# Linear attention's decay levels as differences of one running sum on GpSimd, and the samples' query latents for two heads per product

## What is computed

```python
log_a = jax.nn.log_sigmoid(glr @ w_gate_up + b_gate) / GLA_TAU
...
b = jnp.cumsum(gc, axis=2)
o_inter = jnp.einsum('bhcd,bhde->bhce', qc * jnp.exp(b), state)
diff = b[:, :, :, None, :] - b[:, :, None, :, :]
dec = jnp.exp(jnp.where(causal[None, None, :, :, None], diff, -jnp.inf))
att = jnp.einsum('bhid,bhjd,bhijd->bhij', qc, kc, dec)
...
new_state = jnp.exp(b_last[:, :, 0, :])[..., None] * state + jnp.einsum('bhcd,bhce->bhde', kc * jnp.exp(b_last - b), vc)
...
q_lat = jnp.einsum('bshn,rhn->bshr', q_nope, w_uk)
```

## Time and profile before

| | |
|---|---|
| three timed runs | 752.32, 753.34 (median), 758.79 us |
| the profiled execution | 748.42 us, its span 746.6 us |
| busy share of the span | PE 95%, PE weight load 73%, DVE 48%, ACT 43%, POOL 10% |
| chain that ended last | PE 91%, DVE 3%, ACT 2% |
| granted tensor clock, mean | 0.985 |

### The profile page before, as it was taken

One profiled execution on the slowest core, in us unless ns is written; L12 is line 12 of the kernel. 1 busy time (PEld: TensorE's weight loads), 2 busy tenths in 40 slices (PEclk: granted clock), 3 DMA queues, 4 the chain that ended last, 5 costly groups with the idle time before them and its releaser, 6 DMA issues.

```text
span 746.6 us, 16661 instructions
## 1 busy us (share of the span) xinstructions
PE 706.7 (95%) x7015; PEld 547.9 (73%) x7015; DVE 356.2 (48%) x782; ACT 324.1 (43%) x771; POOL 75.6 (10%) x113
## 2 busy tenths in 40 slices
PE   2899999999999989998899999999999999999995
PEld 1487878788789986776676577676668999668884
DVE  0454370030202024778665766665661112379977
ACT  1244650121212135765566655655757666602100
POOL 0000000000000010101121122012113443000000
PEclk9899999999999997999999999999999999999998
DMA  9996300303001020000010200020655885103332
GB/s 296 396 352 186 113 1 1 113 0 96 0 2 56 2 63 23 15 16 10 10 11 1 46 12 2 1 58 8 217 194 182 288 290 194 60 1 115 119 134 84
DMA packets 35301, 70.31 MB, mean 94 GB/s; under 512 B 6626, under 2 KB 17979, under 8 KB 33564
## 3 DMA queue, kind: packets, MB, share of 16 engines
q1 hardware_dynamic: 30602, 47.73, 19.7%
q0 software_dynamic: 4016, 20.97, 8.0%
q10 hardware_dynamic: 610, 0.55, 0.3%
HBM read 62.26 MB, written 6.07 MB: 92 GB/s over the span
## 4 chain that ended last, share of the span: by engine, by line
PE 91%; DVE 3%; ACT 2%; issue 1%; DMA 1%; ACTq 1%; POOL 0%; DVEq 0%; POOLq 0%
PE banks L2011 15%; PE banks L2023 12%; PE banks L2215 8%; PE banks L2343 5%; PE banks L2424 4%; PE banks L2444 4%; PE banks L2191 3%; PE banks L2577 2%; PE banks L2579 2%; PE banks L2578 2%; PE banks L2129 2%; PE banks L2032 2%; PE banks L2517 2%; PE banks L2536 2%; PE banks L2560 2%; PE banks L2561 1%
## 5 line engine op out<-in xcount | busy, mean ns | idle before, releaser
L1260 ACT ACTIVATE s_z<-banks 128x512 f32<-128x512 f32 (+1 forms) x88 | 41.4, 518 | 48.2 <-PE banks L2424 48.0
L1436 DVE COPY s_zs<-banks 8x512 f32<-8x512 f32 (+3 forms) x6 | 3.5, 576 | 118.5 <-PE banks L1985 118.4
L2011 PE MATMUL banks<-s_w_parts,s_h_b 128*128 128x256 f32 (+3 forms) x296 | 55.5, 315 | 0.0
L1041 ACT ACTIVATE s_z<-banks 128x416 f32<-128x416 f32 (+3 forms) x32 | 14.8, 475 | 92.3 <-PE banks L2011 92.3
L1251 ACT ACTIVATE s_z<-banks,s_temps 128x128 f32<-128x128 f32 (+7 forms) x64 | 47.1, 740 | 5.4 <-DVE s_temps L1738 5.0
L2011 PEld LDWEIGHTS banks<-s_w_parts,s_h_b 128*128 128x128 f32 x296 | 43.3, 189 | 3.6 <-issue 1.7
L2424 PEld LDWEIGHTS banks<-s_ident,s_z 128*128 128x128 f32 x288 | 33.4, 141 | 11.5 <-issue 5.8
L2023 PE MATMUL banks<-s_h_a,s_z_r 128*128 128x512 f32 x128 | 40.8, 395 | 0.0
L2023 PE MATMUL banks<-s_h_b,s_z_r 128*128 128x512 f32 x128 | 40.3, 393 | 0.0
L2424 PE MATMUL banks<-s_ident,s_z 128*128 128x128 f32 x288 | 39.8, 274 | 0.1
L2215 PE MATMUL banks<-s_kt,s_temps 96*128 96x512 f32 (+1 forms) x96 | 39.4, 532 | 0.0
(11 more groups left out here) (401 smaller groups left out, 1569.1 us busy)
## 6 DMA issues: line engine op xcount, KB each, us to landing
s_z<-in_w_ada SPq DMA_DIRECT2D x16, 512.0 KB, 12.1
s_temps<-in_w_in SPq DMA_DIRECT2D x3, 2048.0 KB, 7.9
s_x<-in_x_prompt SPq DMA_DIRECT2D x8, 512.0 KB, 12.0
s_z<-in_w_ada SPq DMA_DIRECT2D x1, 4096.0 KB, 14.1
s_kt<-in_w_out SPq DMA_DIRECT2D x8, 512.0 KB, 4.7
s_temps<-in_x_prompt SPq DMA_DIRECT2D x8, 512.0 KB
out_y_prompt<-s_temps SPq DMA_DIRECT2D x7, 512.0 KB
s_temps<-in_w_in SPq DMA_DIRECT2D x2, 832.0 KB, 14.0
```

The lines of the kernel that those rows point to most:

```text
L1260: nc.scalar.activation(PTb[r % 3][:, 4 * g:4 * g + n, :], banks[:, 4 + (groups(r) + g) % 2, 0:P * n].rearrange("p (j q) -> p j q", j=n), A ...
L2011: last = nc.tensor.matmul(banks[:, proj_bank(c, t), 0:WIDTH[c]], h_[half][:, k, n0:n0 + P], w_, start=(k == 0 and n == 0), stop=(k == KT - ...
```

## The change

The seven levels and the running sum are no longer products. `decay_sums` makes the running sum and the sum behind each token, from `la` itself in fp32: two products of 128 columns by `upto` and one of 256. ScalarE's `sums_out` copies the running sum to SBUF (`cum`) and exponentiates both. GpSimd's `differences` subtracts: per level two operations of 128 elements, the middle's value less the key half, and the query half less the middle's. ScalarE's `levels_out` exponentiates them in place, four levels and then three. The decays and sums have two buffers each. The running sum of block k+2 is now made in iteration k, behind the far products. The gate's bank is 0 from block 2 on, the latent keys' bank is 7. `S` and `attm` are cleared by VectorE. The transfer of the table and its conversion go.

In the samples, `w_uk` is turned for two heads at once (`wT`), the queries of two heads lie in the two halves of the rows with zeros between, and `qlat` is one product for two heads. There is one piece fewer.

```diff
-        ref = col // (2 * s) * (2 * s) + s - 1
-        sums[:, lv] = np.where((col // s) % 2 == 0, (col < row) & (row <= ref), (ref < row) & (row <= col))
-    sums[:, LEVELS] = row <= col
-    c["sums"] = sums.reshape(P, -1)
+    c["upto"] = (row <= col).astype(np.float32)
...
-        k_rows = [carve(256, region=act_flat) for _ in range(2)]
-        ckvT.append(carve(P, region=act_flat))
+        es = [carve((LEVELS + 1) * 256, LEVELS + 1, 2, P, region=act_flat) for _ in range(2)]
+        k_rows = [sb(f"k_rows{i}", [P, 256])[:] for i in range(2)]
...
+            def differences(t):
+                pool.wait_ge(cum_ready, t + 1)
                 if t > 1:
+                    pool.wait_ge(x_ready, t - 1)
+                for lv in range(LEVELS):
+                    n = P >> (lv + 1)
+                    b = halves_of(cum[t % 2], n)
+                    e = halves_of(es[t % 2][:, lv, :, :].rearrange("p h i -> p (h i)"), n)
+                    middle = b[:, :, 0, n - 1:n].to_broadcast([P, P // n, n])
+                    nc.gpsimd.tensor_tensor(e[:, :, 0, :], middle, b[:, :, 0, :], ALU.subtract)
+                    last = nc.gpsimd.tensor_tensor(e[:, :, 1, :], b[:, :, 1, :], middle, ALU.subtract)
+                    if lv in (FIRST_LEVELS - 1, LEVELS - 1):
+                        last.then_inc(diff_ready, 1)
             pool.wait_ge(proj_done, T * (NCH - 1))
             nc.gpsimd.memset(glT, 1.0).then_inc(padded, 1)
-            nc.gpsimd.tensor_copy(after_r, after[:]).then_inc(tables_ready, 1)
-            decay_parts(0)
-            pool.wait_ge(sums_in, 16)
-            nc.gpsimd.tensor_copy(sums, sums_raw).then_inc(tables_ready, 1)
-            decay_parts(1)
-            pool.wait_ge(proj_done, T * NCH)
-            nc.gpsimd.memset(S, 0.0).then_inc(padded, 1)
-            nc.gpsimd.memset(attm, 0.0).then_inc(padded, 1)
-            for t in range(2, T):
-                decay_parts(t)
+            for t in range(T):
+                differences(t)
             pool.wait_ge(kv_out, 32)
...
+            def sums_out(t):
+                act.wait_ge(sums_done, t + 1)
+                if t > 1:
+                    act.wait_ge(diff_ready, 2 * (t - 1))
+                    act.wait_ge(kdec_ready, t - 1)
+                nc.scalar.activation(cum[t % 2], banks[:, 0, 0:256], ACT.Copy).then_inc(cum_ready, 1)
+                nc.scalar.activation(es[t % 2][:, LEVELS, :, :].rearrange("p h i -> p (h i)"), banks[:, 0, 0:256], ACT.Exp, scale=1.0 / TAU).then_inc(sums_ready, 1)
+                nc.scalar.activation(esuf[t % 2], banks[:, 0, 256:512], ACT.Exp, scale=1.0 / TAU).then_inc(sums_ready, 1)
+            def levels_out(t, part):
+                act.wait_ge(diff_ready, 2 * t + part + 1)
+                v = es[t % 2][:, FIRST_LEVELS * part:(FIRST_LEVELS, LEVELS)[part], :, :].rearrange("p l h i -> p (l h i)")
+                nc.scalar.activation(v, v, ACT.Exp, scale=1.0 / TAU).then_inc(e_ready, 1)
...
+                    nc.vector.memset(S, 0.0).then_inc(padded, 1)
+                    nc.vector.memset(attm, 0.0).then_inc(padded, 1)
                     dve.wait_ge(padded, 6)
+                dve.wait_ge(sums_ready, 2 * t + 2)
                 if t > 1:
                     dve.wait_ge(o_done, t - 1)
                     dve.wait_ge(state_done, t - 1)
-                nc.vector.tensor_tensor(qb[t % 2], es[:, LEVELS, :, :].rearrange("p h i -> p (h i)"), kq(t)[:, 256:512], ALU.mult).then_inc(qb_ready, 1)
...
                 if t == 1:
-                    pe.wait_ge(k_copied, 2)
+                    pe.wait_ge(a_copied, 3)
                 for q in range(3):
                     nc.tensor.transpose(banks[:, 6, P * q:P * q + P], z[:, t, P * q:P * q + P], ident[:])
                 nc.tensor.transpose(banks[0:QK, 6, 384:512], z[:, t, W_KR - NOPE:W_GM], ident[:]).then_inc(a_transposed, 1)
             def latent_keys(t):
-                pe.wait_ge(a_copied, 3 * t + 3)
+                pe.wait_ge(a_copied, 3 * t + 1)
+                if t == 0:
+                    pe.wait_ge(la_ready, 2)
+                else:
+                    pe.wait_ge(k_copied, 2 * t)
                 for m in range(H // 2):
-                    last = nc.tensor.matmul(banks[:, 6, P * m:P * m + P], w_uk[:, P * m:P * m + P], turned_latents(t), start=True, stop=True)
+                    last = nc.tensor.matmul(banks[:, 7, P * m:P * m + P], w_uk[:, P * m:P * m + P], turned_latents(t), start=True, stop=True)
                 last.then_inc(k_done, 1)
...
+                nc.tensor.matmul(banks[:, gate_bank(t), 256:512], glT, w_gu[:], start=True, stop=True).then_inc(gate_done, 1)
+            def decay_sums(t):
+                pe.wait_ge(la_ready, t + 1)
+                if t > 0:
+                    pe.wait_ge(sums_ready, 2 * t)
+                for hp in range(2):
+                    nc.tensor.matmul(banks[:, 0, P * hp:P * hp + P], la[t % 2][:, P * hp:P * hp + P], upto[:], start=True, stop=True)
+                nc.tensor.matmul(banks[:, 0, 256:512], after[:], la[t % 2], start=True, stop=True).then_inc(sums_done, 1)
...
+                        if t == 3:
+                            decay_sums(0)
                         if t == 4:
                             key_rows(0)
                         if t == 5:
-                            decays(0, 0)
-                            decays(0, 1)
                             key_rows(1)
+                            decay_sums(1)
                         if t == 6:
-                            decays(0, 2)
-                            decays(0, 3)
-                            decays_after(0)
+                            latent_rows(0)
                             gate_rows(2)
-            latent_rows(0)
             latent_keys(0)
             pe.wait_ge(proj_copied, T * NCH)
             pe.wait_ge(padded, 6)
...
-                if n in (PREP["wT0"], PREP["wT1"]):
-                    for h in range(4):
-                        c0 = NOPE * (4 * (n - PREP["wT0"]) + h)
-                        last = nc.tensor.transpose(banks[0:NOPE, 7, P * h:P * h + P], w_uk[:, c0:c0 + NOPE], ident[:])
+                if n == PREP["wT"]:
+                    for m in range(H // 2):
+                        last = nc.tensor.transpose(banks[:, 7, P * m:P * m + P], w_uk[:, P * m:P * m + P], ident[:])
                 if n == PREP["qT"]:
                     pe.wait_ge(p_q4, 4)
                     for h in range(H):
-                        nc.tensor.transpose(banks[0:NOPE, 7, NB * h:NB * h + NB], sq[:, QK * h:QK * h + NOPE], i8)
+                        rows, c0 = slice(NOPE * (h % 2), NOPE * (h % 2) + NOPE), NB * (h // 2)
+                        nc.tensor.matmul(banks[rows, 7, c0:c0 + NB], sq[:, QK * h:QK * h + NOPE], i8, start=True, stop=True)
                     for h in range(H):
                         last = nc.tensor.transpose(banks[:, 7, 64 + NB * h:64 + NB * h + NB], sq4[:, h, :, :].rearrange("p a e -> p (a e)"), i8)
                 if n == PREP["qlat"]:
-                    for h in range(H):
-                        last = nc.tensor.matmul(banks[:, 7, NB * h:NB * h + NB], w_ukT[:, h, :], s_ql[:, h, :], start=True, stop=True)
+                    for m in range(H // 2):
+                        last = nc.tensor.matmul(banks[:, 7, 2 * NB * m:2 * NB * m + 2 * NB], w_ukT[:, m, :], s_ql[:, m, :, :].rearrange("p a b -> p (a b)"),
+                                                start=True, stop=True)
                 if n == PREP["init"]:
                     for b in range(NB):
                         nc.tensor.matmul(banks[0:32, 7, b:b + 1], qlw[:, b, 24:56], knT[:, b:b + 1], start=True, stop=False)
```

More of the change, by code:

```diff
@@ L246, in hybrid_step @@
         la = [carve(256) for _ in range(2)]
-        la_hi, la_lo = ([carve(256, region=C_parts) for _ in range(2)] for _ in range(2))
-        after_r = carve(P, region=C_parts)
+        cum = [carve(256) for _ in range(2)]
         xs = carve(LEVELS * 256, LEVELS, 256)
-        esuf = carve(256)
+        esuf = [carve(256) for _ in range(2)]
+        ckvT = [carve(P) for _ in range(2)]
         assert taken[0] <= B
-        ckvT = [carve(P)]
         attm = carve(512, 2, 2, P)
@@ L299, in hybrid_step @@
         s_cqT = carve(2 * 32, 2, 32)
-        s_ql = carve(H * NB, H, NB, rows=NOPE)
+        s_ql = carve(H * NB, H // 2, 2, NB)
         s_decT = carve(2 * NB, 2, NB)
@@ L326, in hybrid_step @@
         s_ss = sb("s_ss", [NB, 8])
-        w_ukT = carve(H * P, H, P, rows=NOPE)
+        w_ukT = carve(H // 2 * P, H // 2, P)
         assert taken[0] <= MLA_AT
@@ L619, in turned_latents, with gate_bank @@
             return ckvT[t % 2] if t < SOON else ckvT_late[:, t - SOON, :]
+        def gate_bank(t):
+            return 7 if t < 2 else 0
+        FIRST_LEVELS = 4
         def late_at(s):
```

188 lines of the change are left out of this document (68 added, 120 removed).

## The result

| kernel | time, median us | over the kernel before, 95% interval |
|---|---|---|
| before | 752.83 (749.21 to 758.79, 4 runs) | |
| changed | 760.02 (758.04 to 763.01, 4 runs) | 1.009 (1.0045 to 1.0134) |
| changed, second series (10 runs) | 760.08 | 1.0091 (1.0055 to 1.0127) |

The change costs 0.9%, 6.8 us, where 4.6 less were forecast: outside the range, on the wrong side. The profiled execution of the changed kernel took 759.15 us, 757.3 its span. The page: products went, and TensorE's busy time with them (706.7 to 698.6 us), but the span grew by 10.7, so the engine stands idle instead.

The account below looks back on a forecast made before the run. In the loop TensorE, VectorE and ScalarE were taken as near their limits, with VectorE's ring binding after the change. -1.1 - 2.3 - 3.4 + 3.5 - 0.8 - 0.5 = -4.6 us, from 753.3 to 748.7; range 739.0 to 758.5.

Parts of the forecast that it names:

- (1): Projections: block 0's sums go, the new sums of blocks 0 and 1 come in at 1.0 us each; -1.1 us.
- (2): Entry to the linear-attention loop: TensorE's waits of 0.93 and 1.39 us for ScalarE's copies go; -2.3 us.
- (3): Loop iteration k = 0: full clock wins 2.4 us, products removed 1.0; -3.4 us, to 11.4.
- (4): Loop iterations 1 to 5: VectorE and GpSimd collide, 62.9 us against 59.4; +3.5 us.
- The late ring: Loop, k = 3 to 5: VectorE's queue, each part waiting for the one before, takes 12.3 us per iteration.
- the collision: Loop: VectorE's two-SBUF-input products and GpSimd's differences take turns, 0.60 us a pair against 0.34 for VectorE's products alone.
- The ring of 13.0: Loop, k = 1 and 2: 3.1 us of ScalarE replace log decay and near pairs in VectorE's ring; 13.0 us each.
- (5): Samples' query latents: transposes and latent product records go, narrow products come in; -0.5 us, from -1 to 0.
- No collision: Rival, loop: VectorE and GpSimd do not hold each other up, -5.5 us instead of +3.5; 739.7 us, chance 0.14.
- Dearer GpSimd: Rival, loop: narrow GpSimd operations cost 0.73 us, a pair 0.87, adding 9.5 us; 758.2 us, chance 0.18.
- The clock falls inside the loop: Rival: TensorE's waits, mostly ahead of near products, lower the clock, six falls of 2.4 us; 763.1 us, chance 0.06.
- The entry stays slow: Rival, loop entry: memsets or first differences hold TensorE, clock falls, 2.3 and 2.4 us not won; 753.4 us, chance 0.12.

Follow-up runs that it names:

- the repeat: The changed kernel run and profiled again, nothing altered, beside the runs of its variants: 1.0091 of the kernel before.
- differences apart: Changed kernel with one wait moved: GpSimd's differences start only when VectorE's seven scaled products of the block before are done; 0.9996 of the kernel before.
- both repairs: Changed kernel with GpSimd's differences held behind VectorE's scaled products and the samples' key weights turned in two steps: 0.9918 of the kernel before, 0.9928 again.
- the slots kept: Changed kernel with the samples' key weights turned in two steps, so later sample steps stand in their old slots: 1.0019 of the kernel before.
- experiment 3: Changed kernel with GpSimd's differences held behind VectorE's scaled products, alone (0.9996) and with key weights turned in two steps (0.9918), beside the changed kernel (1.0091).

## Why the prediction was wrong, step by step

**(1), (2) Projections and entry.** Right in kind, smaller in size: -3.4 forecast; the loop began 2.85 us earlier between the first profiles and 1.67 between the second ones (279.35, 277.68). The two waits went, and the memsets, costed at "some tenths", hold TensorE for 1.32.

**(3) Iteration 0.** The time forecast for it, 11.4, came (11.68, and 12.73 in the repeat), by luck. Of the 14.76 us it was compared with, the low clock was 3.5 and not 2.4: at full clock the kernel before takes 11.23, and 5.8 to the far products, not the 6.9 that were taken from k = 1. It has this low clock in two of three profiles of its loop, with the same waits ahead. "The fall came after 2.3 us of idle within 3.5" took one draw for a rule. And the 1.0 us for the products removed was not won: against 11.23, iteration 0 became longer.

**(4) The loop.** Its parts had different fates.
- The late ring, 36.9 us for k = 3 to 5: the number came, 36.1 and 35.9 in the two profiles, by two errors that offset each other. Without the collision these three were to take 31.5 (3 x 10.5) and took 34.3 with the differences apart (34.5 and 33.5 with both repairs); so the collision was 1.6 to 1.8 us there, where 5.4 were counted. The kernel before took 34.9 in one profile and 36.4 in the other.
- The price of GpSimd beside VectorE: right in kind, the wait and the repair alike. A pair takes 0.54 us, not 0.60, and the seven products 1.0 us more, not 1.8. For k = 1 to 5, 9.0 us were forecast (from -5.5 to +3.5). In the traces these five took 66.6, 66.3 and 66.6 us side by side, and 62.4, 61.4 and 60.3 apart: some 5. The timed runs give 7.1 and 7.6 for the whole kernel.
- k = 1 and 2, 26.0 us: wrong, 30.5 and 30.4. The ring of 13.0 holds work of ScalarE and VectorE only (and takes 2.0 us for near pairs whose own row says 2.64). The pauses of 2.2 to 2.7 us in the small products, and the low clock behind them, stand nowhere in the sum.
- The floor under it all is the step that failed. Without the collision the five iterations were to take 53.9 us, 5.5 less than before. Apart they took 62.4, 61.4 and 60.3, against 59.4 and 60.7 before: nothing was won. The sum carries products removed ("1.6 less per block") as time won wherever TensorE binds, and puts the pause at nothing. The row of 0.72 us in the earlier trace rows was read as a pause "that waits for nothing named", and what it would be without the products of 512 columns between the small ones was not asked. It is 1.9 to 2.7 us in five of the seven iterations behind the first.
- Iteration 6, -0.8: nothing came. From its start to the last state product it is 22.1 us in both profiles after, 22.0 and 21.7 before.

**(5) The samples.** -0.5 forecast, +5.1 to +5.9 measured; with the slots kept, the stretch is 0.6 us shorter (180.3 against 180.9). The work was costed rightly and its position not at all: the samples' steps were not followed past the queues that feed them once a removed step moves them. This is the second step that failed.

**The sum.** Forecast -4.6, measured +6.8, 11.4 apart. The slots, put at nothing, are 5.3. The base without collision and with the slots kept was to be -13.6 (-1.1 - 2.3 - 3.4 - 5.5 - 0.8 - 0.5) and is -5.4 and -6.2 in the two series with both repairs, some 7.8 more. The collision was 1.7 too dear.

**Rivals.** "No collision" falls with experiment 3. "Dearer GpSimd" falls: alone, each of a block's fourteen differences but the first two takes 0.40 to 0.46 us in the trace apart (k = 4), at the narrow levels as at the wide, no more than the 455 ns that the forecast took; that its 758.2 us is nearest to the measured 760.0 is chance. "The clock falls inside the loop", with a chance of 0.06, is nearest in kind. It falls in k = 1, 2, 5 and 7 of the first profile, but behind the pauses of the small products and not ahead of the near ones where `scaled` is late; behind the pauses of 1.97 and 1.92 us in k = 4 and 6 it doesn't fall. "The entry stays slow" is partly so, 1.3 us.

Open: whether the pauses are the arrival of instructions, and how much of the loss is the clock's. The low clock comes behind some of these pauses and waits and not behind others like them, and no run held it fixed.

## What to carry to other kernels

A product taken from an engine is worth its time only where nothing else fills the place: look for pauses beside it, even short ones, and ask what they will be when it is gone. Where a list of steps shares slots with other work, a step removed moves all later ones; follow each to what feeds it. And a low clock in one profile may be a draw: take a second profile of the same kernel before it is explained.

## What was not expected of the hardware

- Over 31 runs of the kernel before, the mean granted clock lay between 0.980 and 0.996, and the time fell by 6.0 us per 0.01 of it (line fitted). The changed kernel's mean was 0.975 over 10 runs, against 0.988, apart 0.980, both repairs 0.985. By that line 0.013 of clock is 7.8 us, as much as the change lost. The line shows what goes together, not which is the cause: waits and pauses may lower the clock, and the clock lengthens the work.
- In rows of 216 small products with their loads TensorE pauses, 0.7 to 1.5 us with large products among them and up to 2.7 with fewer. The loop grew by 0.7 to 1.5 us where 7.4 us of products were put into them. In all 41 such pauses of seven profiles it goes on 2.2 to 3.0 us after a piece of the instruction queue has arrived.
- VectorE's 128x256 product and GpSimd's 128x128 difference side by side follow at 0.54 us each, alone at 0.34 and 0.36. The Trainium skill, SBUF — State Buffer, "Who interferes with whom", calls the shared ports an exclusive lock; strictly in turns the pair would take 0.70. The rule's direction holds, its size by these rows is three quarters of that.
